# A hybrid scan and expert-retrieval layer: no zero products, products ahead of the query projection, and fewer products on VectorE

## The reference

```
def peer_ffn(h, w_q, keys1, keys2, u_tab, v_tab):
    ...
    def block(xb):
        q = (xb @ w_q).reshape(PEER_BLOCK, PEER_HEADS, 2, PEER_KEY_DIM // 2).astype(jnp.float32)
        s1 = jnp.einsum('thd,nd->thn', q[:, :, 0], keys1.astype(jnp.float32))
        s2 = jnp.einsum('thd,nd->thn', q[:, :, 1], keys2.astype(jnp.float32))
        ...
        gate = jax.nn.softmax(sc, axis=-1)
        act = jax.nn.gelu(jnp.einsum('thkd,td->thk', u_tab[e], xb), approximate=False)
        return jnp.einsum('thk,thkd->td', gate * act, v_tab[e])
```

## Time and profile before

| what | value |
| --- | --- |
| median of 3 runs | 2748.71 us (2748.07 to 2752.73) |
| the profiled execution | 2741.37 us |
| its span, first to last instruction | 2739.6 us |
| busy: TensorE / VectorE / ScalarE / GpSimd | 2421.6 / 1590.1 / 900.0 / 793.3 us |
| mean granted TensorE clock | 0.968 |
| moved by DMA | 935.29 MB, 687.39 MB of them by GpSimd's gathers |

### The profile page before, as it was taken

How to read it: one execution, slowest core, us unless ns; L and a number is a source line. 1 busy time by engine, 2 the same in 40 slices (tenths; PEclk the granted TensorE clock), 3 DMA queues, 4 the chain that set the end, 5 groups by cost and what they waited for, 6 DMA issues and landing times.

```text
span 2739.6 us, 26850 instructions
## 1 busy us (share of the span) xinstructions
PE 2421.6 (88%) x8530; PEld 1356.4 (50%) x8530; DVE 1590.1 (58%) x3736; ACT 900.0 (33%) x2386; POOL 793.3 (29%) x705
## 2 busy tenths in 40 slices
PE   6999999888998788799898898998998998888786
PEld 3555554356887544455444464443554444334332
DVE  2330012212487775798656798657788557666674
ACT  3100121021122332555424554334644324343332
POOL 0111100000133122343333334334343335444442
PEclk9999999999999889999999999999999999999999
DMA  6222316875898789999999999999999999999996
GB/s 261 100 100 100 115 51 231 328 310 193 314 344 340 280 339 426 406 411 381 426 427 425 425 371 409 426 427 426 413 369 424 423 426 417 427 416 426 426 420 277
DMA packets 143568, 935.29 MB, mean 341 GB/s; under 512 B 16914, under 2 KB 28434, under 8 KB 41026
## 3 DMA queue, kind: packets, MB, share of 16 engines
q0 software_dynamic: 96928, 687.39, 60.8%
q1 hardware_dynamic: 33842, 204.77, 19.1%
q10 hardware_dynamic: 12656, 41.42, 3.8%
HBM read 898.33 MB, written 35.19 MB: 341 GB/s over the span
## 4 chain that ended last, share of the span: by engine, by line
PE 32%; DMA 26%; DVE 12%; ACT 3%; DVEq 2%; issue 2%; POOL 1%; ACTq 1%; POOLq 0%
DMA ring<-in_peer_uv,e_idx 24%; PE e_acc L1803 14%; PE e_acc L1732 5%; DVE ring L1936 5%; PE e_qs L1821 3%; PE e_B L1714 3%; PE e_A L1714 2%; DVEq L1938 2%; DMA e_wb<-in_w_out 1%; POOL ring L1536 1%; ACT e_diag L1652 1%; DMA e_mg<-in_w_late 1%; DVE e_f L1952 1%; PE e_A L948 1%; ACT e_coef L1645 1%
## 5 line engine op out<-in xcount | busy, mean ns | idle before, releaser
L1803 PE MATMUL e_acc<-ring,e_diag 128*128 128x512 f32 x2368 | 1114.8, 618 | 204.7 <-ACT e_diag L1652 204.5
L1536 POOL DMA_INDIRECT ring<-in_peer_uv,e_idx x640 | 753.0, 1177 | 1398.3 <-PE e_acc L1803 1008.8
L1936 DVE CUSTOM_DVE_ANT_0 ring<-ring,e_xb 128x1024 f32<-128x1024 f32 x640 | 774.8, 1224 | 418.9 <-DMA ring<-in_peer_uv,e_idx 397.9
L1803 PEld LDWEIGHTS e_acc<-ring,e_diag 128*128 128x128 f32 x2368 | 448.2, 196 | 785.6 <-issue 481.6
L1642 ACT ACTIVATE e_act<-e_dots 128x2 f32<-128x2 f32 x320 | 65.1, 203 | 734.3 <-DVEq L1938 731.3
L534 PE MATMUL pj<-held,ring 128*128 128x512 f32 x512 | 225.2, 593 | 0.0
L1652 ACT ACTIVATE e_diag<-ident,e_coef 128x128 f32<-128x128 f32 x592 | 206.1, 394 | 20.9
L568 PE MATMUL pj<-ring,held 128*128 128x512 f32 x352 | 156.4, 599 | 10.1 <-DMA ring<-in_w_big 7.9
L1645 ACT ACTIVATE e_coef<-e_act,e_gate 128x1 f32<-128x1 f32 x640 | 153.9, 287 | 23.1 <-issue 1.1
L534 PEld LDWEIGHTS pj<-held,ring 128*128 128x128 f32 x512 | 94.8, 190 | 107.3 <-issue 107.3
L1821 PEld LDWEIGHTS e_qs<-e_h2T,e_w_head 128*128 128x128 f32 x1200 | 141.1, 195 | 10.0 <-issue 9.7
(11 more groups left out here) (405 smaller groups left out, 2338.8 us busy)
## 6 DMA issues: line engine op xcount, KB each, us to landing
e_wb<-in_w_out SPq DMA_DIRECT2D x49, 1024.0 KB, 9.4
ring<-in_w_big SPq DMA_DIRECT2D x18, 2048.0 KB, 9.0
e_w_head<-in_w_q ACTq DMA_DIRECT2D x30, 1024.0 KB, 9.1
ring<-in_w_mod SPq DMA_DIRECT2D x8, 2048.0 KB, 10.3
ring<-in_peer_uv,e_idx POOLq DMA_INDIRECT x640, 12.3
wm<-in_w_mod SPq DMA_DIRECT2D x4, 2048.0 KB, 18.2
e_m<-scratch_mod_rows SPq DMA_DIRECT2D x15, 512.0 KB, 14.7
e_m<-scratch_xbcT SPq DMA_DIRECT2D x7, 1024.0 KB, 14.6
```

The source lines that it names most:

```text
L1536: nc.gpsimd.indirect_dma_start(expert[:, u % RING, :], None, dr["peer_uv"], bass.IndirectOffsetOnAxis(idx[:, h % 4, s:s + 1], 0)).then_inc ...
L1803: mm = nc.tensor.matmul(acc[:, c * 512:(c + 1) * 512], diag[:, v % RING, :], expert[:, v % RING, D + c * 512:D + (c + 1) * 512], start=Fal ...
L1936: nc.vector.tensor_tensor_reduce(expert[:, u % RING, 0:D], expert[:, u % RING, 0:D], xb[p % 2][:, :], 1.0, 0.0, ALU.mult, ALU.add, dots[:, ...
```

## The change

Three edits. (1) `begin` keeps only its wait, `end` is gone: the first product of a block that TensorE makes carries the start flag, the last one the stop flag. The zero tile and `f_mm` are gone (a small tile `ready` still tells TensorE that the constants are there); who takes the sum waits for the last product's count of `slot_free`. (2) In TensorE's body `begin` and the products come first, then the projection (step 0) or the scores (step 2). (3) VectorE makes the products of heads 0 and 1 only; the 16 of heads 2 to 5 go to TensorE, and ScalarE makes a diagonal for each.

```
-ON_VECTOR = [u < 2 * TOPK or u < 6 * TOPK and u % 4 == 0 for u in range(HEADS * TOPK)]
+ON_VECTOR = [u < 2 * TOPK for u in range(HEADS * TOPK)]
...
+FIRST_PRODUCT = [min(u for u in range(SLOTS * p, SLOTS * (p + 1)) if not ON_VECTOR[u]) for p in range(BLOCKS)]
+LAST_PRODUCT = [max(u for u in range(SLOTS * p, SLOTS * (p + 1)) if not ON_VECTOR[u]) for p in range(BLOCKS)]
...
             def block_sum(p):
                 if p:
-                    act.wait_ge(f_mm, p + 1)
+                    act.wait_ge(slot_free, earlier(LAST_PRODUCT[p]) + 1)
...
                 else:
                     pe.wait_ge(late_free, LATE_UNITS)
-                for c in range(2):
-                    nc.tensor.matmul(acc[:, c * 512:(c + 1) * 512], zero[:, :], z512, start=True, stop=False)
-
-            def end(p):
-                for c in range(2):
-                    last = nc.tensor.matmul(acc[:, c * 512:(c + 1) * 512], zero[:, :], z512, start=False, stop=True)
-                last.then_inc(f_mm, 1)
...
                         mm = nc.tensor.matmul(acc[:, c * 512:(c + 1) * 512], diag[:, v % RING, :],
-                                              expert[:, v % RING, D + c * 512:D + (c + 1) * 512], start=False, stop=False)
+                                              expert[:, v % RING, D + c * 512:D + (c + 1) * 512],
+                                              start=v in FIRST_PRODUCT, stop=v in LAST_PRODUCT)
...
             def body(m, n):
                 c = m + 2
+                if m >= 0:
+                    if n == 0 and (m == FIRST_ON_PE or m and m % HP == 0):
+                        begin(m // HP)
+                    products(m, n)
                 if c < HEADS:
                     if n == 0:
...
                         last.then_inc(s_mm, 1)
-                if m >= 0:
-                    if n == 0 and (m == FIRST_ON_PE or m and m % HP == 0):
-                        begin(m // HP)
-                    products(m, n)
-                    if m % HP == HP - 1 and n == GROUPS - 1:
-                        end(m // HP)
...
             def first_sum():
-                dve.wait_ge(f_mm, 1)
+                dve.wait_ge(slot_free, earlier(LAST_PRODUCT[0]) + 1)
```

More of the change, by code:

```diff
@@ L1284, in experts @@
         dots, act_v, coef = sb("dots", [P, 2, TOPK]), sb("act", [P, 2]), sb("coef", [P, 4, 2])
-        diag, zero = sb("diag", [P, RING, P]), sb("zero", [P, P])
+        diag, ready = sb("diag", [P, RING, P]), sb("ready", [P, 1])
         ss, root, rr = sb("ss", [P, 1]), sb("root", [P, 1]), sb("rr", [P, 1])
@@ L1322, in experts @@
         dots_ready, diag_ready = sem("dots_ready"), sem("diag_ready")
-        f_mm, acc_free, ss_ready, ms_ready, root_ready, y_ready, y_out, row_in = (
-            sem("f_mm"), sem("acc_free"), sem("ss_ready"), sem("ms_ready"), sem("root_ready"), sem("y_ready"), sem("y_out"),
+        acc_free, ss_ready, ms_ready, root_ready, y_ready, y_out, row_in = (
+            sem("acc_free"), sem("ss_ready"), sem("ms_ready"), sem("root_ready"), sem("y_ready"), sem("y_out"),
             sem("row_in"))
@@ L1696, in _ @@
             ident = t["ident"]
-            z512 = zero[:, :].unsqueeze(1).to_broadcast([P, 4, P])
             def product(p, i):
@@ L2064, in _ @@
             dve_back_init()
-            nc.vector.memset(zero[:, :], 0.0).then_inc(const_ready, 1)
+            nc.vector.memset(ready[:, :], 0.0).then_inc(const_ready, 1)
             interleave(late, back, scan, merge, prepare, body, finish, body_first=True)
```

## The result

The changed kernel takes 2784.4 us in the median of four runs (2776.3 to 2787.1), the kernel before 2748.8: a ratio of 1.0122, 95% interval 1.0102 to 1.0143, so 28 to 39 us slower. The direction was forecast; the size, +6.3 us with 2768 as the upper end, was not. The profiled execution took 2782.6 us, with a span of 2780.9.

The account below looks back on a forecast made before the run. Expert gathers were taken to bound the kernel, so a change counts by time in which no gather moves. 12.0 - 4 - 1.7 = +6.3 us on the median of 2748.7 gave 2755.0 us, range 2734 to 2768.

Parts of the forecast that it names:

- The order between the boundaries: Heads between block boundaries: the same waits open, but a slack of 6.9 us hides 2 to 3 us: nothing.
- The order at three boundaries: Heads 8, 16, 24: products first cost 4.0 us a boundary, 12.0 in all, bounds 0 to 6.0 each.
- The zeros: Zero products gone: -1.7 us at the kernel's end; 3.44 us of TensorE's time go at each boundary.
- Block 0: First block's scan: 16 products move from VectorE to TensorE, three of them shorten the chain: -4 us.
- part 2's price of the order: Products ahead of projection and scores: 3.4 + 1.7 - 1.1 = 4.0 us a boundary, nothing in heads between.
- I follow the second boundary: Worked through heads 15 and 16: delay 1.55 us from head 15, step 3 of head 16 3.4 us later.
- So I add 1.7 us: Head 16, step 3: the clock falls behind the wait of 3.3 us, adding 1.7 us a boundary.
- The mechanism: ScalarE copies query and scores before diagonals, so TensorE waits: 2.4 us in head 15, 3.3 ahead of head 16's step 3.
- Rival C: Clock also falls ahead of step 1, 3.4 us more at each boundary: +16.5 us, 2765.2 us; chance 0.15.
- a clock below 0.9: Granted clock in the heads around the three boundaries; seeing it would show the forecast wrong and the clock rival right.
- Rival B: Boundaries: slots free 5.5 us earlier, idle transfers of 16.7 us shrink: 2734.6 us at half, 2726.3 at all; chance 0.25.
- The end: Kernel's very end: the closing zero group is on the path, so dropping it gives -1.7 us.

Follow-up runs that it names:

- e11: The changed kernel with the old order (projection and scores first) in heads 6 to 8, 14 to 16 and 22 to 24 only: 2743.9 us.
- e4: The changed kernel with the old order everywhere (projection and scores ahead of products): 2728.3 us.
- e7: The changed kernel, but in steps 1 and 3 ScalarE makes the diagonals ahead of copying the query or the scores: 2730.4 us.
- e9: The changed kernel with two zero matmuls ahead of the diagonal waits of steps 1 and 3 in the nine boundary heads: 2774.6 us.
- e2: The kernel before with one edit, no zero products: 2733.2 us.
- e3: The kernel before with one edit, only 32 products on VectorE: 2744.0 us.

## Why the prediction was right or wrong

**The sum, term by term.** The order between the boundaries, counted as nothing, is 15.6 us (e11 against e4). The order at three boundaries stood in the sum as 12.0 net, that is 12.0 + 3 x 3.44 = 22.3 with the zeros' share taken out; it is 56.1 - 15.6 = 40.5 by the medians; the profiles put 39.5 into the nine heads by first dots, and 32.5 by the last products of each head. The zeros, 1.7 at the end and 10.3 at the boundaries, are 14.3 (10.7 to 19.8 by the interval, which takes in the 12.0). Block 0, -4, is -3.6 (-1.4 to -7.7).

**The step that failed** is part 2's price of the order, in three places. To see them, follow TensorE itself, from the start of one head's last products to the start of the next head's. These rows are the last products of heads 14 and 16 before (head 15's are in the earlier trace rows, head 13's at 1529.80 further down), then of heads 13, 14 and 16 after; head 15's after are the last third of the row at 1638.51 above, from 1645.4 on.

```profile
1576.91 3.70 PE L1803 MATMUL e_acc<-ring,e_diag 128*128 128x512 f32 x8 [1.05 <-ACT e_diag L1652]
...
1671.89 3.70 PE L1803 MATMUL e_acc<-ring,e_diag 128*128 128x512 f32 x8 [0.35 <-ACT e_diag L1652]
```

```profile
1548.43 3.70 PE L1799 MATMUL e_acc<-ring,e_diag 128*128 128x512 f32 x8 [2.09 <-ACT e_diag L1656]
...
1601.02 3.70 PE L1799 MATMUL e_acc<-ring,e_diag 128*128 128x512 f32 x8 [1.04 <-ACT e_diag L1656]
...
1701.80 3.70 PE L1799 MATMUL e_acc<-ring,e_diag 128*128 128x512 f32 x8 [0.36 <-ACT e_diag L1656]
```

| head | before, us | changed, us | more | in the prediction |
| --- | --- | --- | --- | --- |
| 14 | 47.1 | 52.6 | 5.5 | 0 |
| 15 | 42.6 | 44.4 | 1.7 | 1.55 |
| 16 | 52.3 | 56.4 | 4.1 | 2.45 |

- *"I follow the second boundary"*, from head 15 on: head 14 stood outside the sum and loses the most, by both waits and the clock behind them. At the first boundary its like, head 6, lost 6.7 us, at the third head 22 3.0: 15.1 us in all.
- *"So I add 1.7 us"*: in head 16 the clock fell behind the wait of 1.99 us ahead of step 1 too, so 1.7 us more. The wait of 1.1 us that the delay was to eat is half there still (0.52).
- *"In heads between boundaries ... nothing"*: I had taken the time between issue and landing, 12.3 less 5.4 us, for slack. With that latency nearly unchanged after (12.0 in the middle), 31 heads lost 15.6 us by the medians, half a us each on average. The time that gathers spend between issue and landing did not work as a reserve for the engines that release them.

For head 15 the working holds: its delay was to be 1.55 us, because the wait of 1.70 ahead of its last products would shrink, and that wait is gone after. At the three boundaries the nine heads took 33.0 us more by this measure, where the sum has 12.0.

**The mechanism** was right: ScalarE's in-order copies, lengths of the waits, no cover from the products. e7 shows it by itself.

**Rival C** was right in kind. Its price for the clock, 3 x (1.7 + 3.4) = 15.3 us, is near the 15.6 us that the clock column gives for the nine heads, but partly by luck: it counted step 1 of head 15, which kept its 3.70 us, and not head 14, whose two groups took 5.40. Its total fell short by the waits of heads 6, 14 and 22 and of those between boundaries. Its sign, a clock below 0.9, did not come, and the cost did: 0.96 to 0.98 was enough. Against this rival I had set the one row with 2.36 us. The trace of before held another, which I passed over:

```profile
1529.80 5.35 PE L1803 MATMUL e_acc<-ring,e_diag 128*128 128x512 f32 x8 [2.09 <-ACT e_diag L1652]
```

The rule that I weighed there (the Trainium skill, TensorE: Matmul & The Clock Gate, HAM oscillation: waits between groups of matmuls can make each group start at half clock) is borne out in part: of the eighteen groups behind projection and scores in the nine heads, ten took 5.3 to 5.4 us, and in e9 filling the waits with work of no use gave 10 us back.

**Rival B** did not come with this order: in the changed kernel the shares at the boundaries, in windows as far behind the scan's pieces as those of the earlier trace rows, are 0.84, 0.80 and 0.84. But its mechanism, that pause-free work on TensorE opens the gap in the transfers, is real, and the zero products are the work that matters. Without them and in the old order, in e4, the gap nearly closes, against 0.79, 0.70 and 0.78:

```profile
1238.04:1258.04 20.00, 19.86 (x78) 11.96 (x77) 17.97 (x52) 15.43 (x34) 6.90 (x7) 1.00 0.92 342
1623.91:1647.91 24.00, 24.00 (x113) 15.89 (x111) 21.61 (x66) 17.25 (x39) 8.09 (x7) 1.00 0.89 350
2017.15:2041.15 24.00, 23.36 (x87) 13.52 (x86) 21.77 (x69) 18.22 (x44) 9.05 (x8) 1.00 0.91 336
```

e2, with the zeros alone gone, has 0.92, 0.91 and 0.96 there, and e3, which keeps them, 0.79, 0.74 and 0.79. So idle transfers fell from 16.7 us to 0.08 x 20 + 0.09 x 24 + 0.04 x 24 = 4.7 in e2.

**The end** went as worked out. From the last products' start to ScalarE's copy of the sum it was 5.45 us before (first fence), and is 3.74 now:

```profile
2722.66 3.70 PE L1803 MATMUL e_acc<-ring,e_diag 128*128 128x512 f32 x8 [1.21 <-ACT e_diag L1652]
...
2728.11 1.01 ACT L1627 COPY e_f<-e_acc 128x1024 f32<-128x1024 f32 x1 [5.51 <-PE e_acc L1791]
```

```profile
2765.60 3.70 PE L1799 MATMUL e_acc<-ring,e_diag 128*128 128x512 f32 x8 [1.17 <-ACT e_diag L1656]
2769.34 1.01 ACT L1631 COPY e_f<-e_acc 128x1024 f32<-128x1024 f32 x1 [3.79 <-PE e_acc L1799]
```

**Open:** how much of the 14.3 us of the zeros lies where. The profiled executions of before and e2 differ by 8.0 us only (2741.4 and 2733.4). By first dots 6.8 us lie in the nine heads, by last products only 2.0, and the end has 1.7; the 12.0 us of idle transfers that went are near the whole gain, but that they are the gain isn't shown. By which step the losses between boundaries add up was seen only in that e7, with the same order, doesn't have them.

## What to carry to other kernels

When an engine's work is put in another order, follow each result to the in-order engine that handles it, and see what stands ahead of the urgent instruction there: here two copies ahead of two diagonals cost 56 us, and 2 us behind them. Work it through every head that has the same chain, not only those of the stage that looks tight, and price the clock behind each wait, the short ones too. A long wait on another engine, such as VectorE's 30 us here, may be a mirror: take that wait away alone before believing it.

## What was not expected of the hardware

TensorE's clock fell behind a wait of 1.99 us in heads 14 and 16 and held behind one of 2.44 in head 15. In head 22 it held behind the same two waits as in head 14:

```profile
1969.49 3.70 PE L1799 MATMUL e_acc<-ring,e_diag 128*128 128x512 f32 x8 [1.99 <-ACT e_diag L1656]
...
1982.57 3.70 PE L1799 MATMUL e_acc<-ring,e_diag 128*128 128x512 f32 x8 [3.29 <-ACT e_diag L1656]
```

So the length of the wait alone doesn't decide. What does was not tried. Eighteen groups of useless matmuls, 31 us of TensorE's time in the stage that it bounds, made the kernel 10 us faster; the granted clock there was 0.99 to 1.00 with them and 0.96 to 0.98 without.
